# Splitting 520 token columns into 256 and 264 and padding the streamed rows to 544 words

## The chip, the cores and the metric

One core of a Trainium2 chip runs the whole program as one launch. The metric is the device time of that launch in microseconds (us); the time before the change is the median of three runs, 2272.84 us. TensorE appears in the profile as PE (matmuls) and PEld (weight loads), VectorE as DVE, ScalarE as ACT, GpSimd as POOL, SyncE as SP.

## The reference

Two layers of a decoder are run on 512 prompt tokens and 8 sample tokens, which share all weights. All arrays are fp32, the model width is 1024, the hidden width of an FFN 2816.

```python
for i in range(2):
    x = x + 0.5 * rmsnorm(swiglu(rmsnorm(x, g0), wi1, wo1), g1)   # FFN 1
    x = x + rmsnorm(mixer_i(rmsnorm(x, g2)), g3)                  # i=0: attention + short conv; i=1: RG-LRU block
    x = x + 0.5 * rmsnorm(swiglu(rmsnorm(x, g4), wi2, wo2), g5)   # FFN 2
    x = x + (p[i] @ w_pe) * sigmoid(rmsnorm(x, g6) @ w_pg)        # per-layer embedding
```

swiglu is `(silu(g) * u) @ wo` with `g, u = split(x @ wi)`. The prompt goes through causal attention with forget gates, the samples attend to pages of a cache; conv and recurrence states are outputs too.

## The kernel before, in words

The tokens of both groups are columns: every activation is a tile of 128 partitions (features) by chunks by 520 columns (TOK), so x is `[128, 8, 520]`. A product takes 128 output features at a time ("a tile"). Its result goes to one of four accumulators, `acc[0..3]`, each `[128, 2, 512]` in PSUM, that is, two banks of 512 fp32 words. A bank is too small for 520 columns, so the columns are cut in two halves of 260 (HALF): half 0 lies in words 0 to 259 of the first bank, half 1 in words 0 to 259 of the second.

Accuracy is kept by splitting. A weight unit (up to 1 MB, up to 2048 words a partition) is loaded into `raw`; ACT rounds it to `w_hi` in type fp32r (L634, L776), DVE makes `w_lo = raw - w_hi` (L964). Activations are split the same way into `act_hi` (ACT, L666) and `act_lo` (DVE, L1017), hidden ones into `hid_hi` (L704) and `hid_lo` (L1073), the second layer's conv output into `xc_hi` and `xc_lo`, the embedding input into `p_hi` and `p_lo`. `chunk` (L1471 to 1478) then issues six matmuls for each chunk of 128 input features: the products hi by hi, w_lo by act_hi, w_hi by act_lo, each for half 0 and half 1, and each with its own weight load of 128 columns. A tile over 8 chunks is thus 48 matmuls of 260 columns, all at L1475. `k_outer` (L1513) does the same for the first three tiles of a sublayer with the chunk as outer loop, so that it can begin as soon as the first chunk of the activations is split.

```python
for n, (w, m) in enumerate(((w_hi, hi), (w_hi, lo), (w_lo, hi))):
    for half in range(2):
        ins = nc.tensor.matmul(a[0:width, half, 0:HALF], w[slot][:, at:at + width],
                               m[:, half * HALF:(half + 1) * HALF],
                               start=first and n == 0, stop=last and n == 2)
```

Rows of a streamed tile are 520 words, 2080 bytes, apart, and the two halves 1040 bytes. `act_hi` and `act_lo` themselves begin at a multiple of 128 bytes of a partition (by the sizes of the tensors allocated ahead of them), `hid_hi` and `hid_lo` 32 bytes past one. So a stream begins at 32c bytes (plus 32 for the hidden ones) past a multiple of 128 in half 0 of chunk c, and 16 more in half 1. Weights are begun at multiples of 128 bytes, in steps of 512.

The order of the work is written out by hand: a plan lists the units and the jobs (the uses of the accumulators, in turn), every engine walks through it, and semaphores count what is loaded, split, computed and drained. Weight units come over SP's queue into two slots. Three fourths of the matmuls stand in the FFNs, in loops of PE (`pe.Fori`) over pairs of units. DVE and ACT drain an accumulator with one instruction over `acc[:, :, 0:HALF]`, a pattern of two runs of 260; `two` reshapes the other operands, which lie in SBUF, to match: L1063 (the gate and up tiles), L1132 and L1134 (output tiles), the root of the mean square at L659. The norm behind a sublayer is worked in the two halves so that half 0 is begun before the other is there (L1025, L1027). The sums for the norms (L1557, L1560, L1568) are plain fp32 matmuls with `mean_of`, also in halves. The tensors under `y` and under `hid_hi` are overlays: several sets of tensors share one region.

Of the kernel before, what the change touches and what calls it, by code (L numbers as in the profile page):

```python
# [45 lines left out]
TOK = SEQ + DEC  # L46
HALF = TOK // 2
DEPTH = 2
# [211 lines left out]
def trunk(nc, weights, params_d, const_d, x_d, p_d, kpages_d, vpages_d, lfpages_d, table_d,  # L260
# [7 lines left out]
    with ctx:  # L268
# [6 lines left out]
        def overlay(*groups):  # L275

            made, most = [], 0
            for group in groups:
                with ExitStack() as own:
                    made += [own.enter_context(nc.sbuf_tensor(n, s, dt)) for n, s, dt in group]  # L280
                    most = max(most, sum(4 * math.prod(s[1:]) for _, s, _ in group))
            sb("under_" + groups[0][0][0], [P, (most + 63) // 4])
            return made


        x = sb("x", [P, KC, TOK])
        act_hi = sb("act_hi", [P, KC, TOK], F32R)
        act_lo = sb("act_lo", [P, KC, TOK], F32R)
        raw = [sb(f"raw{i}", [P, UNIT]) for i in range(2)]
# [16 lines left out]
        lru = sb("lru", [P, 4 * KC])  # L306
        xr_tail = sb("xr_tail", [P, KC, CC - 1 + DEC])
        y, ring, v_tok, xi = overlay(
            [("y", [P, KC, TOK], F32)],
# [6 lines left out]
         lru_a, lru_v, gt, xc_hi, xc_lo) = overlay(  # L316
            [("hid_hi", [P, HID[0], TOK], F32R), ("hid_lo", [P, HID[0], TOK], F32R),
             ("gs0", [P, TOK], F32), ("gs1", [P, TOK], F32), ("us0", [P, TOK], F32), ("us1", [P, TOK], F32)],
            [("p_raw", [P, PLE_K, TOK], F32), ("p_hi", [P, PLE_K, TOK], F32R), ("p_lo", [P, PLE_K, TOK], F32R),
             ("sig", [P, KC, TOK], F32)],  # L320
# [10 lines left out]
            [("lru_a", [P, KC, TOK], F32), ("lru_v", [P, KC, TOK], F32), ("gt", [P, KC, TOK], F32),  # L331
             ("xc_hi", [P, 4, TOK], F32R), ("xc_lo", [P, 4, TOK], F32R)])
        gs, us = [gs0, gs1], [us0, us1]
# [34 lines left out]
        def cols(ap, half):  # L368
            return ap[:, half * HALF:(half + 1) * HALF]

        def two(ap):
            return ap.rearrange("p (a n) -> p a n", a=2)

# [3 lines left out]
        def tile_of(j):  # L377

            return acc[j % ACCS][:, :, 0:HALF]

# [239 lines left out]
        def _(act):  # L620
# [35 lines left out]
            def statistics(name, rs):  # L656

                wait_job(act, name)
                drains(nc.scalar.activation(two(rs[:, :]), tile_of(J[name]), ACT.Sqrt, bias=eps[:, 0:1]), name)  # L659

# [13 lines left out]
            def begin(s):  # L674
                if s % 4:

                    a = acc_of(f"{s}.post")
                    act.wait_ge(post_half, POSTS.index(s) + 1)
                    nc.scalar.activation(cols(rs_post, 0), a[:, 0, 0:HALF], ACT.Sqrt, bias=eps[:, 0:1])\
                        .then_inc(root_half, 1)  # L680
                    wait_job(act, f"{s}.post")
                    drains(nc.scalar.activation(cols(rs_post, 1), a[:, 1, 0:HALF], ACT.Sqrt, bias=eps[:, 0:1]),
                           f"{s}.post")
# [175 lines left out]
            def recurrent(s):  # L859
# [8 lines left out]
                def gates(c):  # L868
# [5 lines left out]
                    if c:  # L874

                        act.wait_ge(tr_done, c)
                    drains(nc.scalar.activation(two(tr[:, :]), tile_of(J[name]), ACT.Tanh, scale=0.5,
                                                bias=lru[:, 2 * KC + c:2 * KC + c + 1]), name)
# [3 lines left out]
                    if c >= 2:  # L882
                        act.wait_ge(xi_ready, c - 1)
                    drains(nc.scalar.activation(two(ti[:, :]), tile_of(J[name]), ACT.Tanh, scale=0.5,
                                                bias=lru[:, 3 * KC + c:3 * KC + c + 1]), name)
# [66 lines left out]
        def _(dve):  # L952
# [101 lines left out]
            def scaled(out, name):  # L1054

                wait_job(dve, name)
                drains(nc.vector.tensor_tensor(two(out), tile_of(J[name]), two(rs_pre[:, :]), ALU.mult), name)

            def hidden(j, e, gate, up, tile, unit_lo):

                for out, (a, wait, _) in ((gs[e], gate), (us[e], up)):
                    dve.wait_ge(acc_ready, wait)
                    nc.vector.tensor_tensor(two(out[:, :]), acc[a][:, :, 0:HALF], two(rs_pre[:, :]), ALU.mult)\  # L1063
                        .then_inc(drained[a], 1)
# [11 lines left out]
            def last_output(s, name, add):  # L1076

                m = KC - 1
                for half in range(2):
                    src, out = acc_of(name)[:, half, 0:HALF], cols(y[:, m, :], half)  # L1080
# [17 lines left out]
            def ffn(s):  # L1098
                tile0 = FT * (s // 2)
                k0 = 0  # L1100
                for half in range(2):
# [26 lines left out]
                    for m in range(KC):  # L1128
                        name = f"{s}.out{'ab'[half]}{m}"
                        wait_job(dve, name)  # L1130
                        if half == 0:
                            drains(nc.vector.tensor_copy(two(y[:, m, :]), tile_of(J[name])), name)  # L1132
                        elif m < KC - 1:
                            drains(nc.vector.tensor_tensor(two(y[:, m, :]), tile_of(J[name]), two(y[:, m, :]),  # L1134
                                                           ALU.add), name)
                        else:
                            last_output(s, name, True)
# [5 lines left out]
            def mixer_out(s):  # L1143
                for m in range(KC):
                    name = f"{s}.out{m}"
                    wait_job(dve, name)
                    if m < KC - 1:
                        drains(nc.vector.tensor_copy(two(y[:, m, :]), tile_of(J[name])), name)
                    else:
# [4 lines left out]
            def attention(s):  # L1154
                for m in range(AC):

                    name = f"{s}.q{m}"
                    wait_job(dve, name)
                    drains(nc.vector.scalar_tensor_tensor(out=two(q[:, m, :]), in0=tile_of(J[name]), scalar=HD ** -0.5,
                                                          in1=two(rs_pre[:, :]), op0=ALU.mult, op1=ALU.mult), name)  # L1160
                    done(name)
                def key_scores(i):
# [5 lines left out]
                    if i == STEPS - 1:  # L1168
# [8 lines left out]
                wait_job(dve, name)  # L1177
                drains(nc.vector.tensor_tensor(two(z), acc_of(name)[0:HEADS, :, 0:HALF], two(rs_pre[0:HEADS, :]),
                                               ALU.mult), name)
# [251 lines left out]
            def ple(s):  # L1431
                def embedding(m):
# [3 lines left out]
                    dve.wait_ge(sig_ready, KC * (s // 4) + m + 1)  # L1436
                    drains(nc.vector.tensor_tensor(two(sig[:, m, :]), tile_of(J[name]), two(sig[:, m, :]), ALU.mult),
                           name)
# [23 lines left out]
        def _(pe):  # L1462
# [8 lines left out]
            def chunk(a, slot, at, hi, lo, first, last, width=P):  # L1471

                for n, (w, m) in enumerate(((w_hi, hi), (w_hi, lo), (w_lo, hi))):
                    for half in range(2):
                        ins = nc.tensor.matmul(a[0:width, half, 0:HALF], w[slot][:, at:at + width],  # L1475
                                               m[:, half * HALF:(half + 1) * HALF],
                                               start=first and n == 0, stop=last and n == 2)
# [27 lines left out]
            def k_outer(jobs, units, inp, wait_hi, wait_lo, chunks=range(KC), before_last=lambda: None):  # L1505
# [3 lines left out]
                def product(n, c, w, part, start, stop):  # L1509
                    unit = units[n // 2]  # L1510
                    at = (2 * c + n % 2) * P
                    for half in range(2):
                        ins = nc.tensor.matmul(accs[n][:, half, 0:HALF], w[unit % 2][:, at:at + P],  # L1513
                                               part[:, half * HALF:(half + 1) * HALF], start=start, stop=stop)
                    return ins
# [34 lines left out]
            def begin(s, tiles, units):  # L1550
                if s % 4:
# [4 lines left out]
                    for half in range(2):  # L1556
                        nc.tensor.matmul(a[:, half, 0:HALF], mean_of[:, :], cols(ysum, half), start=True, stop=False)  # L1557
                    for half in range(2):
                        pe.wait_ge(ysq7_ready, 2 * n + half + 1)
                        nc.tensor.matmul(a[:, half, 0:HALF], mean_of[:, :], cols(ysq[1], half), start=False, stop=True)\  # L1560
                            .then_inc(acc_ready if half else post_half, 1)
                un = [U[f"{s}.{u}"] for u in units]

                def pre():
                    pe.wait_ge(xsum_added, (KC - 1) * (s + 1))
                    a = claim(J[f"{s}.pre"])
                    for half in range(2):
                        ins = nc.tensor.matmul(a[:, half, 0:HALF], mean_of[:, :], cols(xsum, half),  # L1568
                                               start=True, stop=True)
# [328 lines left out]
```

## Time and profile before

| | us |
|---|---|
| runs | 2274.7, 2269.87, 2272.84 |
| median | 2272.84 |
| profiled execution, first to last instruction (span) | 2269.0 |
| median less span | 3.8 |
| PE busy / PEld busy | 2155.9 / 2094.9 |
| DVE busy / ACT busy / POOL busy | 1142.8 / 696.5 / 214.6 |
| mean granted clock of TensorE | 0.962 of full |

The profile gives no separate device time for the profiled execution; its span is 0.9 us under the fastest of the three runs. Busy PE counts the time in which some matmul is under way, and matmuls overlap: a matmul is shown with about 282 ns while the next begins some 120 ns after it. So the pace of a row of matmuls is read from starts and counts, not from durations. The other figures are read as they stand.

### The profile page before, as it was taken

The page shows a single profiled execution, that of the slowest core. Times are in us where ns is not written, and L with a number is a line of the kernel's source. Part 1 is how long each engine was busy: PE and PEld are TensorE (multiplying, and loading weights), DVE is VectorE, ACT ScalarE, POOL GpSimd, SP SyncE. Part 2 cuts the span into 40 slices and gives each one's busy share as a digit, 9 for nine tenths or more (in the row PEclk, how much of TensorE's full clock was granted, in tenths as well). Part 3 has the DMA queues.
Part 4 walks back from the last instruction along what each step waited for, and adds up shares of the span by engine and source line. Part 5 has one row for each costly group of instructions (what it writes and reads, how often), then busy time and mean ns, then how long its engine had stood idle before and what let it go on. Part 6 is the DMA issues. An engine that isn't in the chain of part 4 may idle for free.

```text
span 2269.0 us, 39498 instructions
## 1 busy us (share of the span) xinstructions
PE 2155.9 (95%) x17060; PEld 2094.9 (92%) x17060; DVE 1142.8 (50%) x1271; ACT 696.5 (31%) x834; POOL 214.6 (9%) x170
## 2 busy tenths in 40 slices
PE   8999999799999899999989999999788899999988
PEld 8999999797868899999979999999788799999978
DVE  6433443854554743344476442443897764334365
ACT  4221222322333322122334221222355332222232
POOL 2000000401110200000043000000322200000021
PEclk9999999987979999999999999999999999999999
DMA  4222222231131222322222222222122222222221
GB/s 170 86 86 98 93 72 96 89 118 56 61 117 67 75 93 70 109 87 77 93 75 75 104 78 96 93 79 91 58 71 95 75 88 82 84 99 93 70 97 66
DMA packets 35726, 197.50 MB, mean 87 GB/s; under 512 B 4760, under 2 KB 5048, under 8 KB 19760
## 3 DMA queue, kind: packets, MB, share of 16 engines
q1 hardware_dynamic: 31680, 183.87, 23.4%
q0 software_dynamic: 3952, 12.28, 1.7%
q8 instruction: 70, 1.15, 0.2%
q14 instruction: 24, 0.20, 0.0%
HBM read 191.68 MB, written 4.46 MB: 86 GB/s over the span
## 4 chain that ended last, share of the span: by engine, by line
PE 86%; DVE 10%; ACT 2%; issue 1%; POOL 0%; DMA 0%; POOLq 0%; DVEq 0%; ACTq 0%
PE acc L1475 77%; PE acc L1513 3%; DVE t L1037 2%; DVE x L1041 2%; DVE act_lo L1017 2%; PE acc L1670 1%; PE acc L1744 1%; DVE w_lo L964 1%; PE acc L1628 1%; PE acc L1710 1%; ACT w_hi L634 1%; PE acc L1730 0%; DVE rs_post L1025 0%; POOL xsum L516 0%; DVE rs_post L1027 0%
## 5 line engine op out<-in xcount | busy, mean ns | idle before, releaser
L1475 PE MATMUL acc<-act_hi,w_hi 128*128 128x260 f32 x3464 | 702.2, 284 | 7.5 <-DVE w_lo L964 6.2
L1475 PE MATMUL acc<-act_hi,w_lo 128*128 128x260 f32 x3464 | 700.4, 284 | 0.0
L1475 PE MATMUL acc<-act_lo,w_hi 128*128 128x260 f32 x3464 | 699.6, 284 | 0.0
L1475 PEld LDWEIGHTS acc<-act_hi,w_hi 128*128 128x128 f32 x3464 | 536.4, 189 | 12.4 <-DVE w_lo L964 9.1
L1475 PEld LDWEIGHTS acc<-act_hi,w_lo 128*128 128x128 f32 x3464 | 535.6, 189 | 0.5
L1475 PEld LDWEIGHTS acc<-act_lo,w_hi 128*128 128x128 f32 x3464 | 534.8, 189 | 0.5
L964 DVE TENSOR_TENSOR w_lo<-raw,w_hi 128x2048 fp32r<-128x2048 f32 (+4 forms) x189 | 380.7, 2014 | 190.1 <-ACT w_hi L634 110.0
L634 ACT ACTIVATE w_hi<-raw 128x2048 fp32r<-128x2048 f32 (+3 forms) x131 | 205.8, 1571 | 363.4 <-PE acc L1475 353.1
L1475 PE MATMUL acc<-hid_hi,w_lo 128*128 128x260 f32 x1408 | 283.0, 282 | 0.0
L1475 PE MATMUL acc<-hid_lo,w_hi 128*128 128x260 f32 x1408 | 283.0, 282 | 0.0
L1475 PE MATMUL acc<-hid_hi,w_hi 128*128 128x260 f32 x1408 | 282.8, 282 | 0.0
L1063 DVE TENSOR_TENSOR us<-acc,rs_pre 128x520 f32<-128x520 f32 x88 | 61.5, 699 | 345.2 <-PE acc L1475 345.2
L1475 PEld LDWEIGHTS acc<-hid_lo,w_hi 128*128 128x128 f32 x1408 | 216.8, 188 | 0.0
L1475 PEld LDWEIGHTS acc<-hid_hi,w_hi 128*128 128x128 f32 x1408 | 216.7, 188 | 0.0
L1475 PEld LDWEIGHTS acc<-hid_hi,w_lo 128*128 128x128 f32 x1408 | 216.6, 188 | 0.0
L776 ACT ACTIVATE w_hi<-raw 128x2048 fp32r<-128x2048 f32 x64 | 122.7, 1918 | 226.6 <-PE acc L1475 226.6
L532 POOL TENSOR_TENSOR w_lo<-raw,w_hi 128x1024 fp32r<-128x1024 f32 x12 | 30.5, 2565 | 1601.3 <-ACT w_hi L634 1601.3
L1513 PE MATMUL acc<-act_hi,w_hi 128*128 128x260 f32 x456 | 75.9, 306 | 64.6 <-ACT act_hi L666 63.1
L704 ACT ACTIVATE hid_hi<-us 128x520 f32 (+1 forms) x88 | 56.4, 641 | 248.4 <-DVE us L1068 248.4
L1513 PEld LDWEIGHTS acc<-act_hi,w_hi 128*128 128x128 f32 x456 | 66.5, 207 | 67.8 <-issue 67.2
L701 ACT ACTIVATE gs<-gs 128x520 f32<-128x520 f32 x88 | 56.4, 641 | 155.1 <-DVE gs L1063 155.1
L1073 DVE TENSOR_TENSOR hid_lo<-us,hid_hi 128x520 f32 (+1 forms) x88 | 61.6, 700 | 83.2 <-ACT hid_hi L704 83.2
(232 smaller groups left out, 1824.8 us busy)
## 6 DMA issues: line engine op xcount, KB each, us to landing
raw<-in_weights SPq DMA_DIRECT2D x122, 1024.0 KB, 4.8
raw<-in_weights SPq DMA_DIRECT2D x32, 768.0 KB, 4.2
raw<-in_weights SPq DMA_DIRECT2D x32, 640.0 KB, 3.9
ring<-in_k_pages POOLq DMA_DIRECT2D x16, 256.0 KB, 3.5
ring<-in_v_pages POOLq DMA_DIRECT2D x16, 256.0 KB, 3.4
raw<-in_weights SPq DMA_DIRECT2D x12, 256.0 KB, 6.4
x<-in_x SPq DMA_DIRECT2D x8, 260.0 KB, 7.2
out_y<-x SPq DMA_DIRECT2D x8, 260.0 KB, 2.0
```

The lines of the kernel that those rows point to most:

```text
L634: nc.scalar.activation(w_hi[slot][:, 0:size], raw[slot][:, 0:size], ACT.Copy).then_inc(hi_ready, 1)
L701: nc.scalar.activation(gs[e][:, :], gs[e][:, :], ACT.Silu).then_inc(silu_ready, 1)
L704: nc.scalar.activation(hid_hi[:, j, :] if isinstance(j, int) else hid_hi[:, j, :].rearrange("p a n -> p (a n)"), us[e][:, :], ACT.Copy).th ...
L776: nc.scalar.activation(w_hi[slot][:, :], raw[slot][:, :], ACT.Copy).then_inc(hi_ready, 1)
L964: nc.vector.tensor_tensor(w_lo[slot][:, 0:size], raw[slot][:, 0:size], w_hi[slot][:, 0:size].bitcast(F32), ALU.subtract).then_inc(lo_ready, 1)
L1017: nc.vector.scalar_tensor_tensor(out=act_lo[:, c, :], in0=x[:, c, :], scalar=pre_gain(s, c), in1=act_hi[:, c, :].bitcast(F32), op0=ALU.mul ...
L1037: nc.vector.scalar_tensor_tensor(out=t[c % 2][:, :], in0=y[:, c, :], scalar=post_gain(s, c), in1=rs_post[:, :], op0=ALU.mult, op1=ALU.mult)\
L1041: nc.vector.tensor_tensor(x[:, c, :], x[:, c, :], t[c % 2][:, :], ALU.add).then_inc(x_ready, 1)
L1063: nc.vector.tensor_tensor(two(out[:, :]), acc[a][:, :, 0:HALF], two(rs_pre[:, :]), ALU.mult)\
L1073: nc.vector.tensor_tensor(pick(hid_lo), us[e][:, :], pick(hid_hi).bitcast(F32), ALU.subtract)\
L1475: ins = nc.tensor.matmul(a[0:width, half, 0:HALF], w[slot][:, at:at + width], m[:, half * HALF:(half + 1) * HALF], start=first and n == 0, ...
L1513: ins = nc.tensor.matmul(accs[n][:, half, 0:HALF], w[unit % 2][:, at:at + P], part[:, half * HALF:(half + 1) * HALF], start=start, stop=stop)
```

## The change

`CUT = 256` takes the place of `HALF = 260`: half 0 is columns 0 to 255, half 1 columns 256 to 519, 264 of them. In PSUM half 0 is written to words 256 to 511 of the first bank and half 1 to words 0 to 263 of the second, so that the 520 results are one run, and `whole` reads them so; `two` is gone. The streamed tiles (`act_*`, `hid_*`, `p_*`, `xc_*`) get rows of `ROW = 544` words, 2176 bytes, 17 times 128, of which 520 are used. Eight words are put ahead of `y`, and the overlay regions are rounded up to 128 bytes, so that every streamed tile begins at a multiple of 128. With 256 columns, 1024 bytes, in half 0, every stream of both halves then begins at a multiple of 128 bytes. The tiles that the plain fp32 matmuls stream (`xsum`, `ysum`, `ysq`) keep their rows. The order of the work, all loops, waits, weights and DMAs and the number of instructions stay.

```diff
-HALF = TOK // 2
+CUT = 256
+ROW = 544
...
-            sb("under_" + groups[0][0][0], [P, (most + 63) // 4])
+            sb("under_" + groups[0][0][0], [P, (most + 127) // 128 * 32])
...
-        act_hi = sb("act_hi", [P, KC, TOK], F32R)
-        act_lo = sb("act_lo", [P, KC, TOK], F32R)
+        act_hi = sb("act_hi", [P, KC, ROW], F32R)[:, :, 0:TOK]
+        act_lo = sb("act_lo", [P, KC, ROW], F32R)[:, :, 0:TOK]
...
+        sb("to_128_bytes", [P, 8])
...
-            [("hid_hi", [P, HID[0], TOK], F32R), ("hid_lo", [P, HID[0], TOK], F32R),
+            [("hid_hi", [P, HID[0], ROW], F32R), ("hid_lo", [P, HID[0], ROW], F32R),
...
         def cols(ap, half):
-            return ap[:, half * HALF:(half + 1) * HALF]
-
-        def two(ap):
-            return ap.rearrange("p (a n) -> p a n", a=2)
+            return ap[:, CUT:TOK] if half else ap[:, 0:CUT]
+
+        def bank(a, half, parts=P):
+
+            return a[0:parts, 1, 0:TOK - CUT] if half else a[0:parts, 0, 512 - CUT:512]
+
+        def whole(a, parts=P):
+
+            return a[0:parts, :, :].rearrange("p a n -> p (a n)")[:, 512 - CUT:512 - CUT + TOK]
...
         def tile_of(j):
 
-            return acc[j % ACCS][:, :, 0:HALF]
+            return whole(acc[j % ACCS])
...
-                    nc.vector.tensor_tensor(two(out[:, :]), acc[a][:, :, 0:HALF], two(rs_pre[:, :]), ALU.mult)\
+                    nc.vector.tensor_tensor(out[:, :], whole(acc[a]), rs_pre[:, :], ALU.mult)\
...
-                        ins = nc.tensor.matmul(a[0:width, half, 0:HALF], w[slot][:, at:at + width],
-                                               m[:, half * HALF:(half + 1) * HALF],
+                        ins = nc.tensor.matmul(bank(a, half, width), w[slot][:, at:at + width],
+                                               cols(m, half),
                                                start=first and n == 0, stop=last and n == 2)
```

The other drains, the root in halves (`bank(a, 0)`, `bank(a, 1)`), `k_outer` and the norm sums are changed in the same way.

## Rows read from the trace of the kernel before

**Rows 1.** The page: busy time by engine, and the granted clock by slice
```profile
span 2269.0 us, 39498 instructions
PE 2155.9 (95%) x17060; PEld 2094.9 (92%) x17060; DVE 1142.8 (50%) x1271; ACT 696.5 (31%) x834; POOL 214.6 (9%) x170
PEclk9999999987979999999999999999999999999999
```
**Rows 2.** The page: the chain that ended last, by engine and line
```profile
PE 86%; DVE 10%; ACT 2%; issue 1%; POOL 0%; DMA 0%; POOLq 0%; DVEq 0%; ACTq 0%
PE acc L1475 77%; PE acc L1513 3%; DVE t L1037 2%; DVE x L1041 2%; DVE act_lo L1017 2%; PE acc L1670 1%; PE acc L1744 1%; DVE w_lo L964 1%; PE acc L1628 1%; PE acc L1710 1%; ACT w_hi L634 1%; PE acc L1730 0%; DVE rs_post L1025 0%; POOL xsum L516 0%; DVE rs_post L1027 0%
```
**Rows 3.** The chain in order of time: start us, us, what; FFN pieces
```profile
32.22 362.85 PE acc L1475 x3024
...
766.50 362.85 PE acc L1475 x3024
...
1233.70 362.88 PE acc L1475 x3024
```
**Rows 4.** Windows, FFN stretches: act tiles first, hid tiles second
```profile
60.00:140.00 80.00, 80.00 (x668) 80.00 (x667) 34.39 (x35) 22.39 (x21) 0.00 (x0) 1.00 0.24 86
160.00:218.00 58.00, 58.00 (x486) 58.00 (x486) 17.73 (x14) 10.86 (x7) 0.00 (x0) 1.00 0.27 93
```
**Rows 5.** The page: groups of DVE that drain or split, idle before, releaser
```profile
L964 DVE TENSOR_TENSOR w_lo<-raw,w_hi 128x2048 fp32r<-128x2048 f32 (+4 forms) x189 | 380.7, 2014 | 190.1 <-ACT w_hi L634 110.0
L1063 DVE TENSOR_TENSOR us<-acc,rs_pre 128x520 f32<-128x520 f32 x88 | 61.5, 699 | 345.2 <-PE acc L1475 345.2
```
**Rows 6.** Timeline of PE, k_outer at half clock: start us, us, xcount
```profile
1214.82 1.50 PE L1513 MATMUL acc<-act_lo,w_hi 128*128 128x260 f32 x6
1216.12 1.50 PE L1513 MATMUL acc<-act_hi,w_hi 128*128 128x260 f32 x6
1217.42 1.50 PE L1513 MATMUL acc<-act_hi,w_lo 128*128 128x260 f32 x6
```
**Rows 7.** Timeline of PE, a tile with weights 8 columns wide, 48 matmuls
```profile
436.29 0.40 PE L1475 MATMUL acc<-act_hi,w_hi 128*8 128x260 f32 x2
...
441.96 0.40 PE L1475 MATMUL acc<-act_hi,w_hi 128*128 128x260 f32 x2
```
**Rows 8.** Timeline of PE, 128-column weight loads with 2 streamed columns
```profile
616.66 3.63 PE L1710 MATMUL acc<-pT,ring 128*128 128x2 f32 x32
```
**Rows 9.** Groups by form, PE: the mean duration of such a matmul
```profile
L1710 PE MATMUL acc<-pT,ring 128*128 128x2 f32 x128 | 15.0, 252 | 0.0
```
**Rows 10.** Timeline of PE, one FFN tile: first matmuls of its chunks
```profile
112.75 0.40 PE L1475 MATMUL acc<-act_hi,w_hi 128*128 128x260 f32 x2
...
113.47 0.40 PE L1475 MATMUL acc<-act_hi,w_hi 128*128 128x260 f32 x2
...
114.19 0.40 PE L1475 MATMUL acc<-act_hi,w_hi 128*128 128x260 f32 x2
...
114.91 0.41 PE L1475 MATMUL acc<-act_hi,w_hi 128*128 128x260 f32 x2
...
115.65 0.40 PE L1475 MATMUL acc<-act_hi,w_hi 128*128 128x260 f32 x2
...
116.37 0.40 PE L1475 MATMUL acc<-act_hi,w_hi 128*128 128x260 f32 x2
```

More of the change, by code:

```diff
@@ L316, in trunk @@
          lru_a, lru_v, gt, xc_hi, xc_lo) = overlay(
-            [("hid_hi", [P, HID[0], TOK], F32R), ("hid_lo", [P, HID[0], TOK], F32R),
+            [("hid_hi", [P, HID[0], ROW], F32R), ("hid_lo", [P, HID[0], ROW], F32R),
              ("gs0", [P, TOK], F32), ("gs1", [P, TOK], F32), ("us0", [P, TOK], F32), ("us1", [P, TOK], F32)],
-            [("p_raw", [P, PLE_K, TOK], F32), ("p_hi", [P, PLE_K, TOK], F32R), ("p_lo", [P, PLE_K, TOK], F32R),
+            [("p_raw", [P, PLE_K, ROW], F32), ("p_hi", [P, PLE_K, ROW], F32R), ("p_lo", [P, PLE_K, ROW], F32R),
              ("sig", [P, KC, TOK], F32)],
@@ L331, in trunk @@
             [("lru_a", [P, KC, TOK], F32), ("lru_v", [P, KC, TOK], F32), ("gt", [P, KC, TOK], F32),
-             ("xc_hi", [P, 4, TOK], F32R), ("xc_lo", [P, 4, TOK], F32R)])
+             ("xc_hi", [P, 4, ROW], F32R), ("xc_lo", [P, 4, ROW], F32R)])
+        hid_hi, hid_lo, p_raw, p_hi, p_lo, xc_hi, xc_lo = (
+            m[:, :, 0:TOK] for m in (hid_hi, hid_lo, p_raw, p_hi, p_lo, xc_hi, xc_lo))
         gs, us = [gs0, gs1], [us0, us1]
@@ L658, in statistics @@
                 wait_job(act, name)
-                drains(nc.scalar.activation(two(rs[:, :]), tile_of(J[name]), ACT.Sqrt, bias=eps[:, 0:1]), name)
+                drains(nc.scalar.activation(rs[:, :], tile_of(J[name]), ACT.Sqrt, bias=eps[:, 0:1]), name)
             def high(s, c):
@@ L678, in begin @@
                     act.wait_ge(post_half, POSTS.index(s) + 1)
-                    nc.scalar.activation(cols(rs_post, 0), a[:, 0, 0:HALF], ACT.Sqrt, bias=eps[:, 0:1])\
+                    nc.scalar.activation(cols(rs_post, 0), bank(a, 0), ACT.Sqrt, bias=eps[:, 0:1])\
                         .then_inc(root_half, 1)
                     wait_job(act, f"{s}.post")
-                    drains(nc.scalar.activation(cols(rs_post, 1), a[:, 1, 0:HALF], ACT.Sqrt, bias=eps[:, 0:1]),
+                    drains(nc.scalar.activation(cols(rs_post, 1), bank(a, 1), ACT.Sqrt, bias=eps[:, 0:1]),
                            f"{s}.post")
@@ L876, in gates @@
                         act.wait_ge(tr_done, c)
-                    drains(nc.scalar.activation(two(tr[:, :]), tile_of(J[name]), ACT.Tanh, scale=0.5,
+                    drains(nc.scalar.activation(tr[:, :], tile_of(J[name]), ACT.Tanh, scale=0.5,
                                                 bias=lru[:, 2 * KC + c:2 * KC + c + 1]), name)
@@ L883, in gates @@
                         act.wait_ge(xi_ready, c - 1)
-                    drains(nc.scalar.activation(two(ti[:, :]), tile_of(J[name]), ACT.Tanh, scale=0.5,
+                    drains(nc.scalar.activation(ti[:, :], tile_of(J[name]), ACT.Tanh, scale=0.5,
                                                 bias=lru[:, 3 * KC + c:3 * KC + c + 1]), name)
@@ L1056, in scaled @@
                 wait_job(dve, name)
-                drains(nc.vector.tensor_tensor(two(out), tile_of(J[name]), two(rs_pre[:, :]), ALU.mult), name)
+                drains(nc.vector.tensor_tensor(out, tile_of(J[name]), rs_pre[:, :], ALU.mult), name)
             def hidden(j, e, gate, up, tile, unit_lo):
@@ L1079, in last_output @@
                 for half in range(2):
-                    src, out = acc_of(name)[:, half, 0:HALF], cols(y[:, m, :], half)
+                    src, out = bank(acc_of(name), half), cols(y[:, m, :], half)
                     ins = nc.vector.tensor_tensor(out, src, out, ALU.add) if add else nc.vector.tensor_copy(out, src)
@@ L1131, in ffn @@
                         if half == 0:
-                            drains(nc.vector.tensor_copy(two(y[:, m, :]), tile_of(J[name])), name)
+                            drains(nc.vector.tensor_copy(y[:, m, :], tile_of(J[name])), name)
                         elif m < KC - 1:
-                            drains(nc.vector.tensor_tensor(two(y[:, m, :]), tile_of(J[name]), two(y[:, m, :]),
+                            drains(nc.vector.tensor_tensor(y[:, m, :], tile_of(J[name]), y[:, m, :],
                                                            ALU.add), name)
@@ L1147, in mixer_out @@
                     if m < KC - 1:
-                        drains(nc.vector.tensor_copy(two(y[:, m, :]), tile_of(J[name])), name)
+                        drains(nc.vector.tensor_copy(y[:, m, :], tile_of(J[name])), name)
                     else:
@@ L1158, in attention @@
                     wait_job(dve, name)
-                    drains(nc.vector.scalar_tensor_tensor(out=two(q[:, m, :]), in0=tile_of(J[name]), scalar=HD ** -0.5,
-                                                          in1=two(rs_pre[:, :]), op0=ALU.mult, op1=ALU.mult), name)
+                    drains(nc.vector.scalar_tensor_tensor(out=q[:, m, :], in0=tile_of(J[name]), scalar=HD ** -0.5,
+                                                          in1=rs_pre[:, :], op0=ALU.mult, op1=ALU.mult), name)
                     done(name)
@@ L1177, in attention @@
                 wait_job(dve, name)
-                drains(nc.vector.tensor_tensor(two(z), acc_of(name)[0:HEADS, :, 0:HALF], two(rs_pre[0:HEADS, :]),
+                drains(nc.vector.tensor_tensor(z, whole(acc_of(name), HEADS), rs_pre[0:HEADS, :],
                                                ALU.mult), name)
@@ L1436, in embedding @@
                     dve.wait_ge(sig_ready, KC * (s // 4) + m + 1)
-                    drains(nc.vector.tensor_tensor(two(sig[:, m, :]), tile_of(J[name]), two(sig[:, m, :]), ALU.mult),
+                    drains(nc.vector.tensor_tensor(sig[:, m, :], tile_of(J[name]), sig[:, m, :], ALU.mult),
                            name)
@@ L1512, in product @@
                     for half in range(2):
-                        ins = nc.tensor.matmul(accs[n][:, half, 0:HALF], w[unit % 2][:, at:at + P],
-                                               part[:, half * HALF:(half + 1) * HALF], start=start, stop=stop)
+                        ins = nc.tensor.matmul(bank(accs[n], half), w[unit % 2][:, at:at + P],
+                                               cols(part, half), start=start, stop=stop)
                     return ins
@@ L1556, in begin @@
                     for half in range(2):
-                        nc.tensor.matmul(a[:, half, 0:HALF], mean_of[:, :], cols(ysum, half), start=True, stop=False)
+                        nc.tensor.matmul(bank(a, half), mean_of[:, :], cols(ysum, half), start=True, stop=False)
                     for half in range(2):
                         pe.wait_ge(ysq7_ready, 2 * n + half + 1)
-                        nc.tensor.matmul(a[:, half, 0:HALF], mean_of[:, :], cols(ysq[1], half), start=False, stop=True)\
+                        nc.tensor.matmul(bank(a, half), mean_of[:, :], cols(ysq[1], half), start=False, stop=True)\
                             .then_inc(acc_ready if half else post_half, 1)
@@ L1567, in pre @@
                     for half in range(2):
-                        ins = nc.tensor.matmul(a[:, half, 0:HALF], mean_of[:, :], cols(xsum, half),
+                        ins = nc.tensor.matmul(bank(a, half), mean_of[:, :], cols(xsum, half),
                                                start=True, stop=True)
```

## The prediction

> **What bounds the kernel now.** I read the page's busy line first: PE is busy 95% of the span, DVE 50%, ACT 31% [rows 1]. Busy time alone proves little for overlapping matmuls, so the chain comes next: 86% of the end's chain is PE, 77% the one line L1475 and 3% L1513, its outer-loop sister [rows 2]. In order of time, each of the four FFNs has one unbroken piece of 3024 matmuls in 362.85 or 362.88 us [rows 3], 119.99 ns each; I show three of them. Within them the pace is the same for both kinds of stream: 668 matmuls touch a window of 80 us, which is (80.00 + 0.28) / 668 = 120.2 ns, and (58.00 + 0.28) / 486 = 119.9 ns for the hidden tiles [rows 4]. The 0.28 us is what one matmul lasts. The drains wait for PE and not the other way round: L1063 stood idle 345.2 us before its 88 instructions, all of it for PE, and L964, the weight split, takes 2.014 us of a unit that lasts PE some 11.5 us (96 matmuls) [rows 5]. So the kernel is bound by how soon one matmul follows another.
>
> **Where those 120 ns come from.** 260 columns at the full 2.4 GHz are 108.3 ns, so 11.8 ns of each 120.1 are something else. At half the clock (1.2 GHz) the same matmuls follow at 1.30 us for six, 216.7 ns [rows 6], exactly 260 columns: nothing is added there. The weight load isn't the cause: where it is 8 columns instead of 128, 48 matmuls take 441.96 - 436.29 = 5.67 us, still 118.1 ns [rows 7]. And 32 pairs of a 128-column weight load with only 2 streamed columns take 3.63 us, of which the last lasts 0.252: 3.38 / 31 = 109.0 ns [rows 8, 9]. So weight loads hold the pace to no better than 109 ns, and at full clock the stream adds some 9 to 11 ns beyond its columns. What it is, the trace doesn't say. One arithmetic fits closely: 1040 bytes lie in nine blocks of 128 bytes at every start this kernel has (0 to 112 bytes past a multiple of 128, in steps of 16, and 112 + 1040 is just nine blocks); nine blocks are 288 columns, and 288 / 2.4 = 120.0 ns. If a stream at full clock pays for whole blocks, 4 columns beyond 256 cost a block. The 118.1 ns of the narrow tile is a little under that, so the fit isn't perfect.
>
> **The change, part by part.**
> - *The start alone* (rows of 544 words). Chunks 0 and 4 begin on a multiple of 128 bytes in half 0 already. Chunks 0, 1 and 2 take 0.72 us for six matmuls, chunk 3 0.74, chunk 4 0.72 [rows 10]: an aligned start shows no gain. I take 0, bounds as for the halves below.
> - *Half 0, 260 to 256 columns, eight whole blocks.* No row has it. The lower bound is the weight load, 109.0 ns [rows 8]; the upper is chunk 3's pace, 0.74 / 6 = 123.3 ns [rows 10]. I take 109.0, since eight blocks would be 106.7 ns, under the weight load: 120.1 - 109.0 = 11.1 ns saved.
> - *Half 1, 260 to 264 columns.* It still needs nine blocks. Lower bound 110.0 ns, its columns at 2.4 GHz, plus the 2.3 that the 109.0 has over 256 columns' time: 112.3. Upper bound 123.3 + 1.7. I take today's pace plus four columns: 120.1 + 1.7 = 121.8, 1.7 lost.
> - *A pair* thus goes from 240.2 to 230.8 ns, 9.4 saved.
> - *How many pairs.* The four FFN pieces have 4 x 1512 = 6048 [rows 3]. L1475 and L1513 are 80% of the chain [rows 2], 1815 us; less 4 x 362.9 = 1451 leaves 364 us, some of it at half clock, where the mean clock 0.962 makes 172 us of the whole span. There 520 columns take 433 ns a pair however they are cut. That leaves 192 to 364 us, 800 to 1500 pairs; I take 1200. Sum: 7250 x 9.4 = 68 us.
> - *Drains.* One run of 520 instead of two of 260, same element count: 0. They lie beside PE [rows 5]; if they were slower by a tenth, 0.07 us a tile against 5.77 us of matmuls would not show. The half-wise norms are 4 columns sooner and 4 later, nanoseconds eight times. Norm sums are fp32, few, 0.
> - *DMAs, waits, queues.* None is added or moved; SP's and POOL's queues issue the same. Weight units are used up 4% sooner. L964 stays at 2.014 of some 11 us, so the cover holds. Behind the sublayers PE still waits for DVE's t, x and act_lo [rows 2], 6% of the chain, which gets no shorter; after the change these are a larger share and are next.
>
> Profiled time: 2269 - 68 = 2201 us; the median of the runs lies 3.8 above the span, so 2205.
>
> The Trainium skill (TensorE: Matmul & The Clock Gate, Back-to-back issue gap) gives N / 2.4 + 2.5 ns at full clock and N / 1.2 at half, whatever the start. The second agrees with [rows 6]; the first would give 110.8 ns where [rows 4] show 120.2, so it lacks what this stream pays. By that rule the sum of two halves is 221.7 ns however 520 is cut, and the change is worth 0.
>
> **The rivals.**
> - *B: both halves fall to their floors.* If the extra is paid for ragged blocks of any kind and an aligned stream pays none, a pair is 109.0 + 112.3 = 221.3, 18.9 saved, x 7250 = 137 us: 2136. For it: the extra is the same in hidden and act tiles though their starts differ, so it may be a matter of both ends. Against it: starts at a multiple of 128 show no gain in [rows 10].
> - *C: nothing changes.* The extra is a fixed cost per matmul or a slower rate per column. Then 520 columns in two matmuls cost the same: 2273, within 5 us. For it: the pace hardly depends on start or tile [rows 4, 10]. Against it: at half clock no fixed cost is seen [rows 6], though a faster clock may lay it bare. The Trainium skill's gap rule, above, lands here too, and so does its page SBUF — State Buffer (Specifications (TRN2): cachelines of 16 bytes), since all streams already begin and end on 16 bytes.
> - *D: slower.* Streams and weight loads read the same memory at once. Today their starts drift against each other from chunk to chunk; afterwards both begin at multiples of 128 every time. If that relation is a bad one, every matmul goes at the worst pace seen, chunk 3's 123.3 ns [rows 10]: (123.3 - 120.1) x 2 = 6.4 ns a pair, 46 us, 2319. It decides as soon as the pair is above 240.2, that is, if the mean of the halves is above 120.1. For it: chunk 3 is 3 ns slower with the same instructions, and narrow weight loads make the pace 2 ns better [rows 7], so the loads do disturb the stream. Against it: chunks 0 and 4, whose half 0 has just this relation, are not slow.
> - *The change doesn't do what it says*: if the tiles' starts were not at 128 but, say, 32 bytes past, the split would still leave half 0 at nine blocks, and this falls under C.
>
> **How the numbers follow.** Forecast A (only half 0 gains, or both gain a part) 0.42; B 0.17; C 0.22; D 0.19. A's own range is 2180 to 2250: 5 to 12 ns a pair, from a block of half the size (6.7 ns) to a half 1 that pays no more than now. What this kernel's measurement can tell from no change is about 0.2%, 4.5 us; C lies within it but for a little, A and B are faster, D slower. So faster 0.60, within 0.2% 0.21, slower 0.19. The range takes in A, C and most of B, and leaves out most of D: 2130 to 2290.
>
> **What would show it.** In the changed profile the four FFN pieces of 3024 matmuls should last about 349 us (115.4 ns a matmul) instead of 362.9; B would make it 335, C 363, D 373. Groups by form will have 256 and 264 columns apart, and the starts in the timeline tell each half's pace: A wants 109 and 122, B 109 and 112. At half clock a pair must stay at 433 ns. L1063's idle time for PE should shrink with the pieces. I am wrong in the mechanism if half 0 gains no more than its 4 columns, 1.7 ns, and wrong in the size if half 1 falls too, or if waits of PE for DVE in the FFNs appear.

## The result, and the profile after

The changed kernel takes 2283.74 us (median of six runs, 2279.98 to 2289.14) where the kernel before, in runs beside it, takes 2273.77: a ratio of 1.0054 with a 95% interval of 1.004 to 1.0069. It is slower by half a per cent. I had forecast 2205 us, 3% faster. The measured time lies in the range I gave, 2130 to 2290 us, but on the other side of no change, and only because that range was wide enough to take in rival C and a part of D.

The page of the changed kernel, which answers to [rows 1, 2]. Lines of the changed kernel are numbered nine higher: L1484 is what was L1475.

```profile
span 2287.3 us, 39498 instructions
PE 2172.5 (95%) x17060; PEld 2110.6 (92%) x17060; DVE 1143.5 (50%) x1271; ACT 695.8 (30%) x834; POOL 210.2 (9%) x170
PEclk9999999987979999999999999999899999999999
...
PE 86%; DVE 10%; ACT 2%; issue 1%; POOL 0%; DMA 0%; POOLq 0%; SPq 0%; DVEq 0%; ACTq 0%
```

The shares are those of before to within a point, and the instruction counts are the same. PE's busy time grew by 16.6 us, while that of DVE and ACT moved by 0.7 and POOL's fell by 4.4. The chain in order of time shows where, against [rows 3]; columns are start us, us, what:

```profile
34.77 365.35 PE acc L1484 x3024
...
775.84 365.35 PE acc L1484 x3024
...
1245.08 365.37 PE acc L1484 x3024
...
1838.70 365.35 PE acc L1484 x3024
```

Each FFN piece takes 365.35 us instead of 362.85, 2.50 more, and 4 x 2.50 is 10.0 us. The medians differ by as much, 2283.74 - 2273.77. The profiled execution is the longest of the six, and its further 8 us over the span of before lie outside these pieces; other executions of the same kernel have spans from 2278.0 us, so I don't explain them. The four pieces of this execution, in contrast, agree to 0.02 us. I read the mechanism from them.

A piece has 1512 pairs of matmuls: 365.35 / 1512 = 241.6 ns, against 240.0 before. The windows of the changed kernel, as [rows 4], show both kinds of tile slower, (80.00 + 0.28) / 665 = 120.7 ns and 58.28 / 482 = 120.9 ns a matmul:

```profile
60.00:140.00 80.00, 80.00 (x665) 80.00 (x664) 33.82 (x35) 21.79 (x21) 0.00 (x0) 1.00 0.24 83
160.00:218.00 58.00, 58.00 (x482) 58.00 (x481) 16.53 (x15) 10.04 (x8) 0.00 (x0) 1.00 0.31 105
```

Starts taken one by one from the trace, at full clock in act tiles, give 119.6 ns from the start of a 256-column matmul to the next start, and 122.1 for one of 264, which add up to the pair; in hidden tiles they are 119.6 and 122.0. The groups of DVE that answer to [rows 5] are those of before: the weight split has the same mean, the drain of one run of 520 lasts the same 699 ns as that of two runs of 260, and its idle time for PE grew with PE's.

```profile
L973 DVE TENSOR_TENSOR w_lo<-raw,w_hi 128x2048 fp32r<-128x2048 f32 (+4 forms) x189 | 380.6, 2014 | 189.8 <-ACT w_hi L643 109.6
...
L1072 DVE TENSOR_TENSOR us<-acc,rs_pre 128x520 f32<-128x520 f32 x88 | 61.5, 699 | 350.4 <-PE acc L1484 350.4
```

Two things had to be found out: why half 0 didn't become quick, and what makes a pair 1.6 ns longer.

### The profile page after: what moved, and what is told of

Same layout as the page of the kernel before. It is cut to its first block, busy times and chain, and to the rows that moved or that the text cites. A ratio compares the mean times of both kernels' runs of the same rounds, so it can differ in the third digit from the quotient of the medians.

```text
span 2287.3 us, 39498 instructions
## 1 busy us (share of the span) xinstructions
PE 2172.5 (95%) x17060; PEld 2110.6 (92%) x17060; DVE 1143.5 (50%) x1271; ACT 695.8 (30%) x834; POOL 210.2 (9%) x170
## 4 chain that ended last, share of the span: by engine, by line
PE 86%; DVE 10%; ACT 2%; issue 1%; POOL 0%; DMA 0%; POOLq 0%; SPq 0%; DVEq 0%; ACTq 0%
PE acc L1484 77%; PE acc L1522 3%; DVE x L1050 3%; DVE t L1046 2%; DVE act_lo L1026 2%; PE acc L1679 1%; PE acc L1753 1%; DVE w_lo L973 1%; PE acc L1637 1%; PE acc L1719 1%; PE acc L1739 1%; ACT w_hi L643 1%; DVE rs_post L1034 0%; DVE rs_post L1036 0%; PE acc L1577 0%
## 5 line engine op out<-in xcount | busy, mean ns | idle before, releaser
L1484 PE MATMUL acc<-act_hi,w_hi 128*128 128x256 f32 (+1 forms) x3464 | 704.9, 285 | 6.9 <-DVE w_lo L973 5.7
L1484 PE MATMUL acc<-act_hi,w_lo 128*128 128x256 f32 (+1 forms) x3464 | 702.1, 284 | 0.0
L1484 PE MATMUL acc<-act_lo,w_hi 128*128 128x256 f32 (+1 forms) x3464 | 700.9, 284 | 0.0
L1484 PEld LDWEIGHTS acc<-act_hi,w_hi 128*128 128x128 f32 x3464 | 538.7, 189 | 11.5 <-DVE w_lo L973 8.0
L1484 PEld LDWEIGHTS acc<-act_lo,w_hi 128*128 128x128 f32 x3464 | 541.1, 189 | 0.5
L1484 PEld LDWEIGHTS acc<-act_hi,w_lo 128*128 128x128 f32 x3464 | 540.0, 189 | 0.5
L1484 PE MATMUL acc<-hid_hi,w_lo 128*128 128x256 f32 (+1 forms) x1408 | 284.9, 284 | 0.0
L1484 PE MATMUL acc<-hid_hi,w_hi 128*128 128x256 f32 (+1 forms) x1408 | 284.8, 284 | 0.0
L1484 PE MATMUL acc<-hid_lo,w_hi 128*128 128x256 f32 (+1 forms) x1408 | 283.8, 283 | 0.0
L1484 PEld LDWEIGHTS acc<-hid_lo,w_hi 128*128 128x128 f32 x1408 | 219.3, 188 | 0.0
L1484 PEld LDWEIGHTS acc<-hid_hi,w_lo 128*128 128x128 f32 x1408 | 219.0, 189 | 0.0
L1484 PEld LDWEIGHTS acc<-hid_hi,w_hi 128*128 128x128 f32 x1408 | 218.2, 189 | 0.0
L785 ACT ACTIVATE w_hi<-raw 128x2048 fp32r<-128x2048 f32 x64 | 122.7, 1917 | 231.1 <-PE acc L1484 231.1
L1522 PE MATMUL acc<-act_hi,w_hi 128*128 128x256 f32 x456 | 78.9, 314 | 66.2 <-ACT act_hi L675 64.7
```

The lines of the kernel that those rows point to most:

```text
L785: nc.scalar.activation(w_hi[slot][:, :], raw[slot][:, :], ACT.Copy).then_inc(hi_ready, 1)
L1484: ins = nc.tensor.matmul(bank(a, half, width), w[slot][:, at:at + width], cols(m, half), start=first and n == 0, stop=last and n == 2)
L1522: ins = nc.tensor.matmul(bank(accs[n], half), w[unit % 2][:, at:at + P], cols(part, half), start=start, stop=stop)
```

## The experiments

**The two parts of the change apart.** First the split alone:

```diff
-ROW = 544
+ROW = 520
```

> The split 256 and 264 with rows of 520 words: half 0 of chunk c begins 32c bytes past a multiple of 128, half 1 at the same offset. If the uniform 128-byte start of all streams is what costs the 0.5% (theory of the starts), this runs like the kernel before: FFN pieces of 3024 matmuls 362.9 us, ratio 1.000. If the uneven split is what costs it (theory of the split), pieces of 365.4 us and a ratio of 1.005. If a block of 128 bytes were paid for, as I forecast, the split alone would already give 349 us a piece.

Then the padding alone, with twice 260 columns:

```diff
-CUT = 256
+CUT = 260
```

> Twice 260 columns with rows of 544 words: half 0 begins at a multiple of 128 in every chunk, half 1 16 bytes past one. Theory of the starts: pieces near 365 us, ratio near 1.005 (half of that if half 1, 16 bytes off, escapes). Theory of the split: 362.9 us, ratio 1.000.

The split alone gives 2272.47 us, a ratio of 1.0004 (0.999 to 1.0018); the padding alone 2269.58 us, 0.9994 (0.998 to 1.0008). Neither moves the time. Both write their results into PSUM as one run of 520, as the change does, so that costs nothing by itself. The first FFN piece of each, split alone ahead of padding alone:

```profile
32.40 363.18 PE acc L1484 x3024
```

```profile
32.42 362.87 PE acc L1484 x3024
```

So 0.3 of the 2.5 us belong to the split, nothing to the padding, and 2.2 us appear only when both are there. Neither of my two theories foresaw that. With both, and only then, every stream of both halves begins at the same place in 128 bytes. (No trace shows an address; here and below the starts are worked out from the sizes of the tensors.) My blocks of 128 bytes are refuted too: with the split alone a quarter of the 256-column streams (chunks 0, 4, 8) have eight of them, in the changed kernel all have, and no piece went toward 349 us. (The expectation above had 349 for the split alone; by its own rule that would take the padding too.)

**What a matmul costs beside its columns.** Two kernels with very uneven halves, all else as in the changed kernel:

```diff
-CUT = 256
+CUT = 512
```

> Halves of 512 and 8 columns, all else as in the changed kernel. Theory of a fixed cost per matmul at full clock (11.6 ns beside the columns): a 512 lasts 512/2.4 + 11.6 = 225 ns, and the 8 behind it at least the 109 ns of a weight load. Theory of a slower rate per column (0.4615 ns): 236 ns. Blocks of 128 bytes and nothing else: 213 to 216 ns. The whole is then some 334 ns a pair against 241.7 and far slower, near 3000 us.

```diff
-CUT = 256
+CUT = 200
```

> Halves of 200 and 320 columns. Fixed cost: 320/2.4 + 11.6 = 144.9 ns, and 200/2.4 + 11.6 = 94.9, which the weight load lifts to 109: 254 ns a pair. Rate: 147.7 and 109. Blocks: 133.3 (320 is ten whole blocks) and 109, 242 to 245 a pair. If fp32r matmuls under 256 columns go at a lower rate, the 200 lasts several times that.

They take 3756.5 and 2397.35 us, in one run each. I had expected near 3000 for the first: more of it ran at half clock, its mean clock is 0.786. The FFN pieces of the kernel with 512 and 8 columns, the third and the fourth:

```profile
1781.64 517.45 PE acc L1484 x3024
...
2667.03 967.68 PE acc L1484 x3024
```

a window inside each, with the granted clock as the third number from the end, full and half:

```profile
1800.00:1900.00 100.00, 100.00 (x587) 87.42 (x586) 30.02 (x30) 19.18 (x18) 0.00 (x0) 1.00 0.18 63
2700.00:2800.00 100.00, 100.00 (x314) 84.77 (x314) 15.01 (x15) 9.57 (x9) 0.00 (x0) 0.50 0.09 32
```

and one of the kernel with 200 and 320:

```profile
32.89 388.12 PE acc L1484 x3024
```

The fourth piece of the first kernel ran wholly at half clock, a stroke of luck: 967.68 / 1512 = 640.0 ns a pair, which at 1.2 GHz is exactly 768 cycles, 512 and 256. In the kernel with 200 and 320 columns most pairs at half clock take 480 ns, exactly 576 cycles, 256 and 320. So a matmul takes the larger of its columns and 256 cycles, and the 256, two cycles for each of the 128 weight columns, are the load that goes on beside it: with weights 8 columns wide they are gone, as shown below. At full clock the same pair takes 517.45 / 1512 = 342.2 ns, 22.2 more than 768 cycles at 2.4 GHz. For 200 and 320 columns it is 388.12 / 1512 = 256.7, 16.7 more than 576 cycles; for twice 260 it is 240.0, 23.3 more than 520. Shared out over the two matmuls the extra is 8 to 12 ns each. The pairs alone don't tell a fixed cost from a rate per column. The rate theory's 147.7 + 109 for 200 and 320 columns is just the 256.7 measured, and its 236 + 109 = 345 for 512 and 8 is 3 too many.

The tile with narrow weights does tell them apart, without the load. Timeline of PE in the 512-column kernel, 8-column weights, at full clock; each line is a pair:

```profile
649.84 0.39 PE L1484 MATMUL acc<-act_hi,w_lo 128*8 128x512 f32 x2
650.09 0.39 PE L1484 MATMUL acc<-act_hi,w_hi 128*8 128x512 f32 x2
650.35 0.39 PE L1484 MATMUL acc<-act_lo,w_hi 128*8 128x512 f32 x2
```

From start to start the 512 columns take 224.9 ns and the 8 take 27.3, together the 0.25 us seen here (single starts taken from the trace). 224.9 - 213.3 = 11.6 ns, just what the theory of a fixed cost said; a rate would have been 236. The same tile in the kernel with 200 and 320 columns:

```profile
463.83 0.40 PE L1484 MATMUL acc<-act_hi,w_hi 128*8 128x200 f32 x2
464.07 0.40 PE L1484 MATMUL acc<-act_lo,w_hi 128*8 128x200 f32 x2
464.31 0.40 PE L1484 MATMUL acc<-act_hi,w_lo 128*8 128x200 f32 x2
```

Here the 200 columns take 91.7 ns from start to start and the 320 take 146.3, 8.3 and 12.9 ns beyond their columns; a rate says 92.3 and 147.7, one fixed cost of 11.6 says 94.9 and 144.9. So neither theory holds for every size. What these tiles show is 8 to 13 ns beyond the columns from 200 to 512 columns, not in proportion to them, and 24 ns for the 8-column matmul. Only the 512 columns speak against a rate, but by 11 ns. My pairs of 334 and 254 ns were short by 8 and 3, since I had the cost on one matmul of the two only; 11.6 on both gives 343, which is right, and 263, which is too long. With full weights the 8-column matmul isn't stretched to 109 ns itself: its start is followed by the next after 27 ns, and the 512's after 315, so the wait for the load stands in the other interval. No loss below 256 columns beyond the weight load showed.

**Where stream and weights lie.** Now the extra 1.6 ns a pair. If stream and weight load disturb each other by their relative address, moving the weights must help those tiles whose relation it changes, and no others. The hidden tensors lie behind the weights and move along:

```diff
+        sb("shift", [P, 16])
         raw = [sb(f"raw{i}", [P, UNIT]) for i in range(2)]
```

> The changed kernel with raw, w_hi and w_lo (and all behind them) 64 bytes further on: act streams still begin at multiples of 128, weights 64 past one; hidden streams move with the weights, so their relation stays. Theory of relation (stream and weight load collide by their relative address): act tiles leave their 120.9 ns a matmul, hidden tiles stay at 120.8. Theory of the uniform stream alone: both stay. Theory of chance (the pattern falls out of the start-up, not the addresses): both may move.

The windows of this kernel, act tiles first, hidden tiles second:

```profile
60.00:140.00 80.00, 80.00 (x669) 80.00 (x668) 34.39 (x35) 22.43 (x21) 0.00 (x0) 1.00 0.25 85
160.00:218.00 58.00, 58.00 (x482) 58.00 (x481) 15.96 (x15) 10.89 (x7) 0.00 (x0) 1.00 0.30 102
```

The act tiles went from 665 to 669 matmuls in their window, 120.7 to 120.0 ns. The hidden ones kept exactly 482. Its four FFN pieces all took 363.76 us, which is what 1968 act matmuls at 120.0 ns and 1056 hidden ones at 120.8 make:

```profile
33.90 363.76 PE acc L1485 x3024
```

The act streams stayed where they were and changed their pace; the hidden streams moved by 64 bytes and kept theirs. That is what the theory of relation said, and the stream's own place alone can't explain it. Chance would have to fall alike in all four pieces. The edit moves more than the weights, though: DVE, ACT and the DMAs write behind the shift too. Two readings of the traces point to the weight load. Where DVE, ACT and POOL are all idle, a pair in act tiles still takes 240.9 ns in the changed kernel and 238.8 in the 16-byte kernel below. And in the tile with narrow weights the slow layout of 80 bytes below is no slower than the fast one of 16, 235.4 against 235.8 ns a pair, where with full weights it is 241.1 against 238.9. The DMAs' writes weren't separated. The kernel took 2271.36 us in its one run.

Three other layouts, in one run each. All streams 16 bytes past a multiple of 128:

```diff
-        act_hi = sb("act_hi", [P, KC, ROW], F32R)[:, :, 0:TOK]
-        act_lo = sb("act_lo", [P, KC, ROW], F32R)[:, :, 0:TOK]
+        act_hi = sb("act_hi", [P, KC, ROW], F32R)[:, :, 4:4 + TOK]
+        act_lo = sb("act_lo", [P, KC, ROW], F32R)[:, :, 4:4 + TOK]
...
-            m[:, :, 0:TOK] for m in (hid_hi, hid_lo, p_raw, p_hi, p_lo, xc_hi, xc_lo))
+            m[:, :, 4:4 + TOK] for m in (hid_hi, hid_lo, p_raw, p_hi, p_lo, xc_hi, xc_lo))
```

> The changed kernel with every streamed row used from word 4, so that all streams begin 16 bytes past a multiple of 128, as uniformly as before. Theory that uniformity costs: FFN pieces stay near 365.4 us. Theory that the multiple of 128 itself is the bad relation: pieces fall to about 363. Blocks of 128 bytes, my forecast, would make half 0 pay a ninth block here and the piece longer by 20 us than the changed kernel's.

Rows of 528 words:

```diff
-ROW = 544
+ROW = 528
```

> 256 and 264 with rows of 528 words, 2112 bytes: both halves of a chunk begin at a multiple of 128 in even chunks and 64 past one in odd ones. If the cost comes from the chunks' walk in steps of 128 over 512 bytes (period of four chunks in the starts), the finer walk averages it out, about 363 us a piece; if an aligned start is itself bad, half the chunks are, about 364; if it is the split of 256 with any alignment to 64, 365.

The halves in the other order:

```diff
-CUT = 256
+CUT = 264
```

> Halves in the other order, 264 and then 256 columns, rows of 544 words: half 0 begins at a multiple of 128, half 1 32 bytes past one. If it takes both halves at the same offset from 128 (uniform starts) for the 0.5%, the pieces go back to about 363 us; if a 256-column stream with padded rows is enough, they stay at 365.4.

Their first FFN pieces, in that order:

```profile
32.58 361.19 PE acc L1484 x3024
```

```profile
33.89 367.05 PE acc L1484 x3024
```

```profile
33.74 362.89 PE acc L1484 x3024
```

Sixteen bytes turn the slowest but one into the fastest, 361.19 us a piece and 2264.72 us in its run; the theory that the multiple of 128 is the bad place said about 363, so its sign was right and its size short, and uniformity as such costs nothing. My blocks of 128 bytes would have made this piece 20 us longer. With 528-word rows, where chunks alternate between 0 and 64 bytes, I expected 363 to 365 and got 367.05 (2296.31 us): a finer walk doesn't average the cost out, it is the slowest of these layouts. With 264 columns first, half 1 begins 32 bytes past, and the piece is back at 362.89 (2269.26 us), 120.0 ns a matmul, though half 0 is aligned and half 1 has 256 columns.

**More places, and the fast one timed.** The last four kernels use the edit of the 16-byte kernel with other words (8, 12 and 20 in place of 4), and run that kernel again.

> The kernel with all streams 16 bytes past a multiple of 128, timed in rounds. Theory of relation: its FFN pieces of 361.2 us repeat to 0.1 us, and with 1.65 us saved in each of four, plus as much again in proportion outside them, the median is 0.2 to 0.4% below the kernel before: ratio 0.997. Theory of chance: the pieces come out elsewhere between 361 and 366 us, and the ratio with them.

> Streams begin 32 bytes past a multiple of 128, weights at multiples of 128. Theory of relation: another fixed value of the piece, the same in act and hidden tiles; I expect 361 to 364 us, that is, no more than 120.3 ns a matmul. If the walk over 512 bytes matters and not the place in 128, it is 365.4 as in the changed kernel.

> 48 bytes past a multiple of 128. Relation: between 361 and 364 us a piece, act and hidden tiles alike. If only 16-byte steps within 32 bytes mattered, this equals the 361.2 us of the 16-byte offset.

> 80 bytes past a multiple of 128, 16 past one of 64. If the relation has a period of 64 bytes, this equals the 16-byte offset, 361.2 us a piece; if of 128, it has a value of its own.

| start of every stream past 128 | FFN piece, us | ns a matmul | median, us | ratio and interval |
|---|---|---|---|---|
| 0 (the change) | 365.35 | 120.8 | 2283.74 | 1.0054 (1.004 to 1.0069) |
| 16 | 361.19 | 119.4 | 2264.68 | 0.9966 (0.9951 to 0.9981) |
| 32 | 362.86, one of 362.08 | 120.0 | 2269.32 | 0.9996 (0.9983 to 1.0008) |
| 48 | 362.07 | 119.7 | 2270.95 | 1.0003 (0.999 to 1.0016) |
| 80 | 364.55 | 120.6 | 2282.78 | 1.0055 (1.0038 to 1.0072) |

The act tiles of the kernel with shifted weights add the place 64, 120.0 ns. The third column divides a piece by its 3024 matmuls. First pieces of the 16, 32, 48 and 80 byte kernels:

```profile
32.39 361.19 PE acc L1484 x3024
```

```profile
32.26 362.86 PE acc L1484 x3024
```

```profile
33.45 362.07 PE acc L1484 x3024
```

```profile
32.32 364.55 PE acc L1484 x3024
```

The 16-byte kernel repeats its first piece to the last digit in a second trace, and is 0.34% faster than the kernel before, so it beats both kernels of this case. Its windows hold 672 and 488 matmuls, where [rows 4] have 668 and 486:

```profile
60.00:140.00 80.00, 80.00 (x672) 80.00 (x672) 34.40 (x35) 22.38 (x21) 0.00 (x0) 1.00 0.24 85
160.00:218.00 58.00, 58.00 (x488) 58.00 (x487) 17.74 (x14) 10.85 (x7) 0.00 (x0) 1.00 0.27 91
```

80 is not 16, so the relation has no period of 64 bytes; I had offered that as a possibility. 48 is not 16 either.

I had expected act and hidden tiles of the 32-byte kernel to go at one pace. They don't. Its windows, act and hidden tiles in the first FFN piece and then the same two in the third:

```profile
60.00:140.00 80.00, 80.00 (x668) 80.00 (x667) 34.39 (x35) 22.40 (x21) 0.00 (x0) 1.00 0.25 86
160.00:218.00 58.00, 58.00 (x488) 58.00 (x487) 17.71 (x14) 10.87 (x7) 0.00 (x0) 1.00 0.28 94
1256.60:1336.60 80.00, 80.00 (x672) 80.00 (x671) 34.39 (x35) 22.37 (x21) 0.00 (x0) 1.00 0.24 85
1356.60:1414.60 58.00, 58.00 (x484) 58.00 (x484) 17.74 (x14) 10.85 (x7) 0.00 (x0) 1.00 0.26 91
```

By single starts the act tiles go at 120.3 ns a matmul in the first piece and 119.4 in the third, the hidden ones at 119.5 and then 120.3, with the same addresses throughout. So at 32 bytes there are two paces, 0.8 ns apart, and something other than the relation picks one of them; no run shows what. That step is as large as the one which the shift of the weights made. At 0 the pace is 120.8 ns in the act and the hidden tiles of all four pieces, and in the hidden ones of the shifted kernel, so there it goes with the relation. But the table's values are what these traces held, not constants of an offset.

The paces of single chunks, six matmuls each, say the same. In the changed kernel they go round in fours, 119.8, 122.1, 122.7 and 118.7 ns a matmul in the first piece's act tiles, but in the third piece the first act tiles begin that round with 122.7: the same chunk, at the same addresses, is slow in one piece and not in the other. So the row of matmuls falls into a rhythm of its own, whose phase the addresses don't set; that the relation decides which rhythms there are fits all this, but isn't shown.

The order of the medians isn't quite that of the pieces: the 48-byte kernel's pieces are 0.8 us shorter than before, yet its median is the same. What such runs do outside the FFN pieces differs by more than that from one execution to the next.

## Why the prediction was wrong

**What bounds the kernel** was right. The chain, the pace of the matmuls and the idle drains were the right rows, and the whole difference is in that pace.

**Half 0, from 260 to 256 columns** is the step that failed. I took 109.0 ns, because eight blocks of 128 bytes would be quicker than a weight load. It measures 119.6 ns, and even in the best layout, 16 bytes, 117.1. By my own sign, a gain of no more than 1.7 ns, the mechanism was wrong. The fit of nine blocks to 120.0 ns was an accident. What stands in its place is an extra of 8 to 13 ns per matmul at full clock that doesn't fall away at 256 columns, 11.6 for 512 columns with narrow weights; that was rival C, though neither of its forms, a fixed cost or a rate, fits every size. The rows already held a warning that I noted and passed over: the narrow tile at 118.1 ns [rows 7] was below what nine blocks allow.

**Half 1** at 121.8 ns was right: 122.0. So the gain was wrong by one term, nearly whole: of the 11.1 ns that I gave half 0 only 0.5 came. The pair came out at 241.6 instead of 230.8.

**The start alone**, taken as 0 from [rows 10], was right as far as it went: the padding alone gives 0.9994. But I bounded the parts one by one, and the loss is in their coming together. Before, the start of a stream moved by 16 bytes from half to half and 32 from chunk to chunk, so a tile met many relations and got their mean. The change picked a single one within 128 bytes for all streams, 0, and this is a poor one.

**Rival C** gave the first half of the story, the cost that stays, but not the 0.5%. **Rival D** named the mechanism that the runs bear out best, stream and weight load at an address relation that no longer drifts. Its price was too high: 6.4 ns a pair from chunk 3 against 1.65 measured, (365.35 - 362.85) / 1512. Chunk 3 is slow in every act tile of before, 122.5 ns in the mean, but no row of matmuls keeps to its worst chunk: those of the changed kernel, too, lie 4 ns apart. And its counter-argument was weak: an aligned half 0 beside an unaligned half 1 says little, as the padding alone and the swapped halves show at 120.0 ns. **Rival B** is out.

**Drains, DMAs and waits** held: nothing there changed, and at half clock a pair is 433 ns as before, 213 and 220 by starts. **The count of pairs** was low: L1475 and L1513 have 15024 and 1440 matmuls in the trace of before, 8232 pairs, of which 2184 stand outside the pieces, where I took 1200. With a gain of nothing that didn't matter. The rule that I set against the trace (the Trainium skill, TensorE: Matmul & The Clock Gate, Back-to-back issue gap; the page calls it the gap of an isolated matmul) gave this change 0: the split alone bears that out, 1.0004, but it has nothing for the 0.5% of the whole change. At half clock it is right. Its constant of 2.5 ns is not this kernel's: the runs show 11.6 for 512 columns. The measurement decides there.

What stays open is how the extra cost arises, what picks one of the two paces at 32 bytes, and why 0, 80 and the mixed 0 and 64 are poor relations and 16 a good one. The weights' shift shows that the relation matters; no run shows how the memory is arranged. Relations from 96 up weren't tried.

## What to carry to other kernels

A number that fits to 0.1% is no mechanism as long as every row has the same count of the thing it counts: here each stream had nine blocks, so no row could contradict. Look for a size that varies, or hold the forecast near no change. And where two access streams run side by side for thousands of instructions, treat their relative address as a parameter to be measured, since aligning both can pick a poor relation; an offset of 16 bytes was worth 0.9% between two otherwise equal kernels (ratios to the kernel before of 1.0054 and 0.9966).

## What the runs showed of the hardware beyond that

- A matmul in fp32r with its own load of 128 weight columns takes the larger of its column count and 256 cycles, at half clock exactly: 640.0 ns for a 512 and an 8 together, 480 for a 200 and a 320. A split of 520 into two parts of which one is under 256 thus loses: 200 and 320 cost 256.7 ns a pair against 240.0.
- At full clock more comes on top: with narrow weights 8.3 ns for 200 columns, 12.9 for 320, 11.6 for 512. With full weights none shows at half clock.
- With the relative address of stream and weights modulo 128 bytes the mean pace of a piece moves between 119.4 and 120.8 ns, and mixed relations reach 367.05 / 3024 = 121.4.
- In the 32-byte kernel three FFN pieces took 362.86 us and one 362.08 with the same instructions and addresses, so such a row of matmuls has more than one steady pace; act and hidden tiles had changed places between 119.4 and 120.3 ns:

```profile
761.58 362.86 PE acc L1484 x3024
...
1228.85 362.08 PE acc L1484 x3024
```
